# Row slots of a weight ring that wait for less, a first modulation in two halves, and another home for one tile's scores

## The reference, cut to what matters

```
mod = silu(c) @ w_mod + b_mod            # six parts of 1024: shift, scale, gate (attention); shift, scale, gate (ffn)
h   = rmsnorm(x, norm_attn) * (1 + sc_a) + sh_a
q, k, v, dn_q, dn_k, dn_v, z, b, a = split(h @ w_in)
x  += g_a * (concat(diff_attention(q, k, v), gated_delta_net(...)) @ w_out)
h   = rmsnorm(x, norm_ffn) * (1 + sc_f) + sh_f
# PEER: 8 heads, two halves of 128 keys, 16 best of each, 16 best of the pairs -> 128 experts per token
act  = gates * gelu(h . expert_u[idx])   # 128 rows of 1024 per token
x   += g_f * sum(act * expert_v[idx])    # 128 more rows of 1024 per token
y    = rmsnorm(x, norm_out)
```

## Time and profile before

| what | value |
|---|---|
| median of 3 runs | 1592.37 us (1590.33 to 1596.22) |
| the profiled execution | 1579.69 us |
| its span, first to last instruction | 1577.7 us |
| PE, DVE, POOL, ACT busy | 865.6, 813.6, 749.9, 277.6 us |
| granted clock of PE, mean share of full speed | 0.77 |
| bytes moved | 486.09 MB, 404.28 MB of them by POOL's gathers |
| mean rate over the span | 308 GB/s |

### The profile page before, as it was taken

One profiled execution on the slowest core, in us unless ns is written; L12 is line 12 of the kernel. 1 busy time (PEld: TensorE's weight loads), 2 busy tenths in 40 slices (PEclk: granted clock), 3 DMA queues, 4 the chain that ended last, 5 costly groups with the idle time before them and its releaser, 6 DMA issues.

```text
span 1577.7 us, 14365 instructions
## 1 busy us (share of the span) xinstructions
PE 865.6 (55%) x4990; PEld 500.8 (32%) x4990; DVE 813.6 (52%) x2047; ACT 277.6 (18%) x662; POOL 749.9 (48%) x794
## 2 busy tenths in 40 slices
PE   4999998799567776787620675400442005500254
PEld 2566867556353355543210651000110001100010
DVE  2443234687484277851597146897515760087301
ACT  4234443122241232421000020000100000000000
POOL 0001000453446644456676226676667666676663
PEclk9998999899798999899755887655685557755576
DMA  9234446995659988799999729999999999999996
GB/s 394 91 140 151 161 167 254 375 390 215 240 182 356 343 310 316 241 395 352 364 404 357 297 72 375 359 397 364 354 376 376 402 346 335 359 402 364 347 368 234
DMA packets 120295, 486.09 MB, mean 308 GB/s; under 512 B 13344, under 2 KB 14240, under 8 KB 115616
## 3 DMA queue, kind: packets, MB, share of 16 engines
q0 software_dynamic: 111056, 404.28, 68.4%
q1 hardware_dynamic: 9168, 80.90, 13.2%
HBM read 482.50 MB, written 2.62 MB: 307 GB/s over the span
## 4 chain that ended last, share of the span: by engine, by line
DVE 17%; issue 17%; PE 14%; POOL 13%; DMA 6%; another core or an unknown queue 4%; ACT 1%; POOLq 0%; DVEq 0%; ACTq 0%
PE bank L1357 13%; DVE big L2086 11%; POOL big L988 10%; DMA big<-in_ev,idx 2%; POOL big L977 2%; DMA big<-in_ev,rowT 2%; DMA big<-in_eu,consts 2%; DVE hT L2086 1%; POOL hT L988 1%; PE bank L1363 1%; PE bank L1475 0%; DVE big L1876 0%; DVE dn_tok L1970 0%; DVE sq L2112 0%
## 5 line engine op out<-in xcount | busy, mean ns | idle before, releaser
L2086 DVE CUSTOM_DVE_ANT_0 big<-big,hnow 128x1024 f32<-128x1024 f32 x315 | 377.4, 1218 | 193.2 <-DMA big<-in_eu,consts 127.9
L1357 PE MATMUL bank<-big,W 128*32 128x512 f32 x1296 | 259.7, 835 | 167.6 <-DMA big<-in_ev,idx 64.0
L977 POOL DMA_INDIRECT big<-in_eu,consts x236 | 223.4, 947 | 103.4 <-issue 71.6
L988 POOL DMA_INDIRECT big<-in_ev,rowT x197 | 190.5, 967 | 153.5 <-PE bank L1357 76.6
L1357 PE MATMUL bank<-hT,wring 128*128 128x128 f32 (+1 forms) x896 | 143.3, 319 | 40.4 <-issue 32.2
L1363 PE MATMUL bank<-consts 128*128 128x128 f32 x6 | 2.4, 392 | 294.3 <-DVE consts L2101 294.3
L1357 PEld LDWEIGHTS bank<-big,W 128*32 128x32 f32 x1296 | 53.4, 136 | 332.3 <-issue 319.7
L988 POOL DMA_INDIRECT big<-in_ev,idx x118 | 111.7, 947 | 68.2 <-issue 33.3
L1357 PEld LDWEIGHTS bank<-hT,wring 128*128 128x128 f32 x896 | 120.4, 202 | 64.6 <-issue 41.4
L1357 PE MATMUL bank<-big 128*128 128x128 f32 x720 | 100.1, 288 | 40.6 <-issue 23.0
L977 POOL DMA_INDIRECT big<-in_eu,idx x79 | 75.1, 951 | 99.1 <-DVE coef L2086 57.4
(11 more groups left out here) (294 smaller groups left out, 1379.8 us busy)
## 6 DMA issues: line engine op xcount, KB each, us to landing
wring<-in_wch SPq DMA_DIRECT2D x29, 2048.0 KB, 9.2
big<-in_wch SPq DMA_DIRECT2D x6, 1536.0 KB, 8.8
big<-in_eu,consts POOLq DMA_INDIRECT x236
big<-in_ev,rowT POOLq DMA_INDIRECT x197
tok<-in_wch SPq DMA_DIRECT2D x6, 512.0 KB, 9.9
big<-in_ev,idx POOLq DMA_INDIRECT x118
xs<-in_x SPq DMA_DIRECT2D x1, 1536.0 KB, 6.6
out_y<-xs SPq DMA_DIRECT2D x3, 512.0 KB
```

The lines of the kernel that those rows point to most:

```text
L977: nc.gpsimd.indirect_dma_start(row(slot), None, eu, bass.IndirectOffsetOnAxis(ap=idx[t][:, n:n + 1], axis=0)).then_inc(rows_in[slot], 16)
L988: nc.gpsimd.indirect_dma_start(row(slot), None, ev, bass.IndirectOffsetOnAxis(ap=rowT[t][:, n:n + 1], axis=0)).then_inc(rows_in[slot], 16)
L1357: return nc.tensor.matmul(out, lhsT, rhs, start=first, stop=last)
L2086: V.tensor_tensor_reduce(row(slot), row(slot), hnow[:, :], 1.0, 0.0, ALU.mult, ALU.add, coef[t % 2][:, n:n + 1]).then_inc(dot_ready, 1)
```

## The change

1. `row_free` and the planner: slots 12 to 15 wait only for the deferred chunks that lay in half 0 of `wring` (c = 0 and 2), slots 16 to 19 only for those in half 1 (c = 1 and 3).
2. The first four modulation chunks hold parts 0, 2, 1, 3 (`MOD_PART`): shift and scale for features 0 to 511 first. `scales(0)` and `modulate` become two halves each; `channels(0)` waits for half 0 before its first four `k`, for half 1 before the others.
3. Tile 1's first-half scores move to `ops[:, 2048:3072]`, beside the second half's. SP no longer waits for `ids_ready(1, 0, q)` before the load of `nout`.
4. `STAGES`: the slots 21 to 24 serve the first 16 gathers only, not the first 24.
5. `SCALE` and `EARLIER` get other numbers.

```diff
+MOD_PART = (0, 2, 1, 3) + tuple(range(4, 12))
-STAGES = [(16, [8, 9, 10, 11, 20, 21, 22, 23, 24]), (24, [8, 9, 10, 11, 20, 21, 22, 23, 24]), (48, [8, 9, 10, 11, 20]), ...
+STAGES = [(16, [8, 9, 10, 11, 20, 21, 22, 23, 24]), (48, [8, 9, 10, 11, 20]), ...
+def ring_of(c):
+    return RING_OF[CHUNK_NO[token_chunk(c, 1)]]
-EARLIER: ('top_key', 0, 0): 50.0, ('coef', 1, 0): 200.0, ('query', 3, 1): 200.0, ('resid', 0, 1): 15.0, ('top_key', 2, 0): 100.0, ...
+EARLIER: ('top_key', 0, 0): 150.0, ('coef', 1, 0): 100.0, ('query', 3, 1): 150.0, ('resid', 0, 1): 200.0, ('top_key', 2, 0): 30.0,
+         ('query', 1, 1): 30.0, ('query', 3, 2): 30.0, ('experts', 2, 1, 0): 200.0, ('h_turn', 1): 100.0, ...
-SCALE: 'score': 0.8
+SCALE: 'score': 1.0, 'v_batch': 1.0, 'mod': 1.0
...
-    for w in range(2):
-        add(("scales", w), ("DVE", 0.3), after=[("mod_turn", (3, 9)[w])])
-    add(("modulate", 0), ("ACT", 0, 3.0, ("modulate",)), after=[("scales", 0), ("x_turn", 0, 0)])
-    add(("modulate", 1), ("DVE", 0, 5.0, ("modulate",)), after=[("scales", 0), ("x_turn", 0, 1), ("x_turn", 0, 2)])
+    for half in range(2):
+        add(("scales", 0, half), ("DVE", 0.3), after=[("mod_turn", 2 * half + 1)])
+        add(("modulate", 0, half), ("ACT", 0, 1.6, ("modulate", half)), after=[("scales", 0, half), ("x_turn", 0, 0)])
+        add(("modulate", 1, half), ("DVE", 0, 2.5, ("modulate", half)), after=[("scales", 0, half), ("x_turn", 0, 1), ("x_turn", 0, 2)])
...
-            return (xo[:, hh, :], (xo[:, 1, :], ops[:, 3072:4096])[hh], ops[:, 1024 * hh:1024 * hh + 1024])[t]
+            return (xo[:, hh, :], ops[:, 2048 + 1024 * hh:3072 + 1024 * hh], ops[:, 1024 * hh:1024 * hh + 1024])[t]
...
             sp.wait_ge(*squares.at(1, 2))
-            for q in range(2):
-                sp.wait_ge(*ids_ready.at(1, 0, q))
             sp.dma_start(xo[:, 1, :], nout).then_inc(nout_in, 16)
...
                     if slot < ROWS + 8:
                         for c in DEFER:
-                            pool.wait_ge(*product.at("tok", c, 2))
+                            if ring_of(c) == (slot - ROWS) // 4:
+                                pool.wait_ge(*product.at("tok", c, 2))
...
                 for k in range(KD):
+                    if c == 0 and k % 4 == 0:
+                        pe.wait_ge(*modulated0.at(k // 4))
+                        pe.wait_ge(*modulated.at(2, k // 4))
```

More of the change, by code:

```diff
@@ L340, in layer_steps @@
         add(("mod_turn", m), ("PE", 0, 0.9, ("mod_turn", m), 1), ("DVE", 0.25), after=[("mod", m)])
-    for w in range(2):
-        add(("scales", w), ("DVE", 0.3), after=[("mod_turn", (3, 9)[w])])
-    add(("modulate", 0), ("ACT", 0, 3.0, ("modulate",)), after=[("scales", 0), ("x_turn", 0, 0)])
-    add(("modulate", 1), ("DVE", 0, 5.0, ("modulate",)), after=[("scales", 0), ("x_turn", 0, 1), ("x_turn", 0, 2)])
-    mixed = [("modulate", 0), ("modulate", 1)]
+    add(("scales", 1), ("DVE", 0.3), after=[("mod_turn", 9)])
+    for half in range(2):
+        add(("scales", 0, half), ("DVE", 0.3), after=[("mod_turn", 2 * half + 1)])
+        add(("modulate", 0, half), ("ACT", 0, 1.6, ("modulate", half)), after=[("scales", 0, half), ("x_turn", 0, 0)])
+        add(("modulate", 1, half), ("DVE", 0, 2.5, ("modulate", half)), after=[("scales", 0, half), ("x_turn", 0, 1), ("x_turn", 0, 2)])
+    mixed = [("modulate", t, half) for t in range(2) for half in range(2)]
     for b in range(12):
@@ L516, in expert_steps @@
         elif slot >= ROWS:
-            after += [("query", 3, 0), ("h_turn", 0)] + [("token", c, 2) for c in DEFER if slot < ROWS + 8]
+            after += [("query", 3, 0), ("h_turn", 0)] + [("token", c, 2) for c in DEFER if slot < ROWS + 8 and ring_of(c) == (slot - ROWS) // 4]
         elif slot < 8:
@@ L1051, in by_feature, with modulate @@
                 return ins
[L1053 to L1057, removed]
+            def modulate(half):
+                ks = range(4 * half, 4 * half + 4)
+                act.wait_ge(*scl_ready.at(0, half))
+                act.wait_ge(*hT_ready.at(0, 0, half))
+                by_feature(0, 0, ks, hT[:, 0, 4 * half:4 * half + 4]).then_inc(*modulated0.next(half))
             def channels(b):
@@ L1713, in mod_turn, with scales @@
                 dve.wait_ge(*product.at(*job))
-                V.tensor_tensor(modT[:, 4 * m:4 * m + 4, :], ps(*job)[:, 0:8].rearrange("p (i v) -> p i v", v=2),
-                                col(Q[:, Q_BMOD + 4 * m:Q_BMOD + 4 * m + 4], 2), ALU.add
+                n = 4 * MOD_PART[m]
+                V.tensor_tensor(modT[:, n:n + 4, :], ps(*job)[:, 0:8].rearrange("p (i v) -> p i v", v=2),
+                                col(Q[:, Q_BMOD + n:Q_BMOD + n + 4], 2), ALU.add
                                 ).then_inc(*reads(mod_ready, (m,), *job))
-            def scales(w):
-                dve.wait_ge(*mod_ready.at((3, 9)[w]))
+            def scales(w, half=None):
+                dve.wait_ge(*mod_ready.at(9 if w else 2 * half + 1))
@@ L1720, in scales @@
                 q = (Q_NA, Q_NF)[w]
-                V.scalar_tensor_tensor(out=scl[:, w, :, :], in0=modT[:, 24 * w + 8:24 * w + 16, :], scalar=1.0,
-                                       in1=col(Q[:, q:q + 8], 2), op0=ALU.add, op1=ALU.mult
-                                       ).then_inc(*scl_ready.next(w))
-            def modulate():
-                dve.wait_ge(*scl_ready.at(0))
+                a, n = (0, 8) if w else (4 * half, 4)
+                V.scalar_tensor_tensor(out=scl[:, w, a:a + n, :], in0=modT[:, 24 * w + 8 + a:24 * w + 8 + a + n, :], scalar=1.0,
+                                       in1=col(Q[:, q + a:q + a + n], 2), op0=ALU.add, op1=ALU.mult
+                                       ).then_inc(*scl_ready.next(w, half))
@@ L1732, in modulate @@
                 for t in (1, 2):
-                    V.tensor_tensor(hT[:, t], hT[:, t], col(modT[:, 0:KD, 1], P), ALU.add
-                                    ).then_inc(*modulated.next(t))
+                    V.tensor_tensor(hT[:, t, ks], hT[:, t, ks], col(modT[:, ks, 1], P), ALU.add
+                                    ).then_inc(*modulated.next(t, half))
             def channels(b):
```

23 lines of the change are left out of this document (12 added, 11 removed).

## The result

The changed kernel's median is 1598.5 us (1592.09 to 1608.37, 20 runs) beside 1593.88 us (1586.23 to 1600.3, 20 runs) of the kernel before: ratio 1.0034, 95% interval 1.0019 to 1.005. I forecast 1583.4. It is slower by 5 us and not faster by 9: outside the noise of its interval, though inside the 8 us that I had called "no change". Its profiled execution took 1598.75 us and its span is 1596.6. The profiled execution of before was 14 us under its own median, so the 19 us between the two spans overstate the change.

The account below looks back on a forecast made before the run. PE was taken to bind up to the first gathers, transfers from 935 to 1559 us, with holes between. Terms -4.0 (halves) and -5.0 (ring), the rest 0, gave -9.0: 1583.4 us from 1592.37; own range 1579 to 1588, overall 1561 to 1602.

Parts of the forecast that it names:

- the tables: New planner numbers moving instructions inside PE, DVE and ACT: taken as 0, with -27 and +9 us kept for the range.
- the second hole: POOL's wait of 53.95 us, 881.5 to 935.5 us, for tile 1's first value batch, while PE does queries.
- The halves: First modulation split so PE starts `channels(0)` earlier: 4.0 us gained, bounds 2.3 to 8.2, carried to the first gathers.
- The ring wait: Slots 12 to 15 fill from 394.6, not 402.4 us; four gathers move: 5.0 us gained, bounds 0 to 5.0.
- that pause: PE issuing nothing from 411.4 to 428.69 us, beside the gather burst; expected to come earlier with the burst.
- Home of the scores and SP's wait: Tile 1's scores moved to other space and SP's wait dropped before loading the gain: cost and gain 0.
- five slots from gather 16: Gathers 16 to 23 get five slots, not nine: 6 us later at gather 24, covered before gather 48, so 0.
- the slower one: Rival: a burst stops PE in the last deferred product for 17.3 us; 1605.7 us, range 1596 to 1609, chance 0.14.
- The fast one: Rival: tile 1's batches pass three queries of tile 2, 27 us more gained; 1556 us, range 1553 to 1577, chance 0.21.
- the sum that follows from it: If pauses need not move with the burst, as the page implies: -4.0 to -9.0 us, with no preference.

Follow-up runs that it names:

- e4: The changed kernel with the three old tables (`STAGES`, `SCALE`, `EARLIER`) put back: 1586.75 us, ratio 0.9971 to the kernel before.
- e5: The kernel before with the three new tables and no structural edit: 1605.08 us, ratio 1.0063.
- e6: The kernel before with the modulation in halves and the new ring wait in POOL's program, old tables, old order of every engine: 1584.53 us, ratio 0.993.
- e13: The changed kernel with at most four gathers under way for gathers 128 to 159 alone: 1576.15 us, ratio 0.9947 to the kernel before.
- e1: The kernel before with the first modulation in two halves and nothing else: 1591.62 us, ratio 1.0005.
- e2: The kernel before with the new ring wait in POOL's program alone, the planner not told, order kept: 1584.71 us, ratio 0.996.
- e3: The kernel before with the new ring wait in POOL's program and in the planner, which reorders steps; old tables: 1589.79 us, ratio 0.9995.

## Why the prediction was wrong

*The failed step is the tables*: "They move instructions inside PE, DVE and ACT. Where it matters is the second hole ... I take 0, and keep -27 and +9 for the range." They cost about 10 us (e4 against the changed kernel: 10 by the ratios, 11.8 in medians of two sessions; e5 alone: 11). Without that term the sum is right: e6 measures -9.4 against -9.0. I named this step as the likeliest to fail, yet looked for it in the wrong place: the hole at 881 us nearly kept its length (54.9 us, now 52.4). The loss arises between 550 and 571 us: the new order lets POOL issue 18 gathers there without a break, not 8, and they stop PE in the middle of a chain. e13 shows it: with that order and the burst held down, the loss is not there.

*The halves*: forecast 4.0 within 2.3 to 8.2. From DVE to ACT 2 to 3.5 us (9.9 to 10.9 in e1, the changed kernel and e6, against 12.9 and 13.4). The first gather shows nothing beyond its scatter: 275.3 in e1 and 277.3 in e6, which have the halves, against 276.6 in before and 277.6 in e2. Right in mechanism and at the low end in size at the modulation; that they reach the gathers is not shown, and no median shows them by themselves.

*The ring wait*: "exactly four gathers move" holds, with the wait of some 3 us behind them being 7.08, because the replanned order delays the second product. That 5.0 us are kept agrees with e2 (6 us, 2 to 10 by its interval), though its profile doesn't show where. But the replanning that comes with the edit seems to take 5 back (e3), a part of the edit that I did not price.

*"I take that pause to belong to the burst and to come earlier with it"*: it belongs to the burst; it did not simply move. In the changed kernel PE's 17.32 us at 411 us shrank to 5.56, and a pause of 11.14 came at 551.

*Home of the scores and SP's wait, five slots from gather 16*: taken at 0. Nothing contradicts it; they were not run alone. From the first gather to gather 24 it takes 55.5 us in the changed kernel and 53.9 in e5, against 52.8 before, so 1 to 3 us more and not my 6, and the wait before gather 48 still covers them (14.35 us).

*The rivals*: the slower one had the right mechanism (a burst stops PE where the new order has it) and the wrong place, the last deferred product; that 1598.5 us falls into its range is luck. The fast one, the batches before the queries, did not occur: the order there is that of before.

The Trainium skill's page "SBUF — State Buffer" says in the section "SBUF: two separate sides" that the ports of PE and ACT "never wait on anyone", and in "Who interferes with whom" that DMA never contends with a compute engine. I gave the sum that follows from it a sentence and kept the link between burst and pause in the forecast. The runs show the link on the usual chips: with at most four gathers under way the pauses are gone and the medians fall, and with five the long one is back. They don't show what PE waits for, at SBUF or at something else on the way, so the page may be right about SBUF and still mislead here.

What stays open: which resource it is, and whether the recording of semaphore updates has a part in it; which of the moved steps lets the burst grow (no run moves one alone); whether the tables cost anything else (with the cap the two orders differ by 4 us, within their intervals); whether the short cap gains with the old order too; why one chip makes the same transfers faster.

## What to carry to other kernels

When a tuned order is changed as a side effect of an edit, price the new order and not only the edit: run the edit with the old order beside it. A slot that comes free earlier is no gain by itself: it can lengthen a burst. A pause of PE that the profile gives to nothing, beside back-to-back gathers and a DMA share of 1, is a cost to be removed and not a given; limiting the gathers under way to four, which is one wait on a landing, brought the changed kernel 2.4 to 2.8% below the one before on three chips, far more than the change itself. Such a limit has a narrow optimum (three make the kernel 3.6% slower than the one before) and depends on the chip: on the unlike one a cap of four costs 4 to 5%, and 14% where it holds to the end. Measure it on more than one chip.

## What the runs showed of the hardware that was not expected

- On the usual chips a run of gathers issued every 1.25 us without a break goes with stops of PE, of ACT's reads of its products, and of DVE behind them, and a cap of four under way takes the stops away. In the kernels without a cap they are up to 17 us at 411, 6 to 11 us at 551 and 6 to 11 more at 561 with the new tables, and 35 to 63 us in the queries, ended between 849 and 905 us. In the changed kernel the last two matmuls of a query were issued from 804.45 on, and PE's next began at 864.25. ACT's read of that query and SP's next chunk, which wait for it too, started together at 863.55:

```profile
804.45 0.47 PE L1364 MATMUL bank<-hT,wring 128*128 128x128 f32 x2 [0.45 <-issue]
863.55 0.33 SPq L860 DMA_DIRECT2D wring<-in_wch  x1
863.55 0.60 ACT L1009 ACTIVATE dn_tok<-bank 128x512 f32<-128x512 f32 x1 [90.27 <-remote]
864.25 2.04 PE L1364 MATMUL bank<-skr,dn_tok 128*128 128x128 f32 x8 [59.33 <-issue]
```

- What came late there is the signal of a product, not the issue of its matmuls: the trace has the update of PE's semaphore at 863.53, 58.6 us behind the modelled end of the last matmul, 804.92. Whether the product itself was late it doesn't tell.
- A pause is paid for in PE's clock too: behind the 11.14 us the granted clock was 0.50 (1.2 GHz) until 580 us and 0.61 from 580 to 590, and twelve matmuls took 2.90 us and not 1.58.
- The same kernel took 1425 us on one chip and 1582 to 1594 on four others (medians).
